# A PEER transformer block on one core: eight more early down products, low parts moved inside a head, the last two up products by token block

## The chip, the core and the metric

The kernel runs on one core of one Trainium2 chip. TensorE (PE) multiplies, ScalarE (ACT) copies and applies functions, VectorE (DVE) does elementwise work and the sorted lists, GpSimd (POOL) does elementwise work and issues indirect DMAs, SyncE (SP) issues plain DMAs. Each engine works through its own list of instructions in order; engines wait for each other on semaphores. The metric is the device time of one launch in microseconds.

## The reference

One block of a streaming encoder: a token mixer (window attention and gated units, not touched here), then a PEER channel mixer on 512 tokens of width 1024:

```python
q = (xt @ w_query).reshape(T, PEER_HEADS, 2, D_HALF)          # 8 heads, two halves of 128
s = jnp.einsum('thpd,hpnd->thpn', q, sub_keys)                 # 128 keys for each half
top_s, top_i = lax.top_k(s, PEER_TOPK)                         # 16 of 128, each half
cand = top_s[:, :, 0, :, None] + top_s[:, :, 1, None, :]       # 16 x 16 sums
best_s, best_c = lax.top_k(cand.reshape(T, 8, 256), PEER_TOPK) # the picks of a head
ids = i1 * N_KEYS + i2                                         # 128 of 16384 experts a token
gates = softmax(best_s)
a   = jnp.einsum('tkd,td->tk', expert_down[ids], xb)
act = gelu(a) * gates
y   = jnp.einsum('tk,tkd->td', act, expert_up[ids])
x   = x + gt2 * rms_norm(y, g)
```

## The kernel before

**Dense for three blocks, gathered for one.** The tokens lie in four blocks of 128. For the first three (384 tokens) the kernel multiplies with all experts, in 128 tiles of 128 experts: a *down product* (`multiply_down`, n = 0 to 127) gives a tile's activations, gelu follows, they are multiplied with the dense gate matrix of the picks, and an *up product* (`multiply_up`) adds the tile's output into six PSUM banks. Each float32 operand is split into a high part (`dhi`, `uhi`, `ahi`, a rounding copy on ScalarE) and a low part (`dlo`, `ulo`, `alo`, a subtraction on VectorE), and a product is three matmuls for each pair of parts: a down product is 24 matmuls of 384 columns, an up product 18 of 512. For the fourth block the 128 picked rows of each token are gathered by GpSimd, one pick at a time (`gather_down`, `gather_up`); VectorE makes a dot product (`dot`) and adds a weighted row into y (`add_up`), in groups of `SLOTS` = 3 picks (`gathered`).

**Heads.** For head h, TensorE makes queries and scores in two halves; VectorE sorts them. `halves(h)` takes the 16 best of each half (`top16`), `sums(h)` the 16 best of the sums, then adds up the chosen keys of head h - 1 (`select`), and ends with the numbers `pairf` of head h (signal `dve_pair`). GpSimd's `weigh_hits(h)` waits for `dve_pair`; it makes two differences, then `split_wq(h + 2, 1)`, the low part of the query weights that TensorE needs for the second half of the queries of head h + 2, then two products, then `split_wq(h + 3, 0)`. TensorE's order in a head, and ScalarE's, with two early down products:

```python
def head(h, first=False):                # TensorE
    for s in range(2):
        queries(h, (s,))
        multiply_down(2 * h - 2 + s, s, first=first)
    scores_of(h, (0, 1))
# ScalarE: query copies, query weights' high parts, early(2h-2+s), score copies, hits(h-1)
```

Down product n needs `dlo` of n. There are two buffers for each kind of tile: the high part of tile n + 2 (`down_hi` in `early(n)`) waits until down product n has ended, and the load of tile n + 2 (`next_down(n)` on SyncE) waits for the low part of tile n. `store_gel(n)`, which keeps an early tile's gelu in DRAM, stands behind `next_down(n)` in SyncE's list and waits for gelu n. So the load of tile n + 3 is behind gelu n.

**Picks.** After the last head VectorE makes the softmax and the last sums, ScalarE an exp and `hits(7)`, TensorE three sets of transposes. **Gates.** 24 turns (`gates_turn`) follow: two gate products and one early down product a turn; ScalarE copies the gates to `stage` and stores them to `gates_dram` in six chunks of 64 tokens, the last chunk in four stores. Before the change 46 tiles are early: 16 in heads, 6 around the picks (`BETWEEN`), 24 in the gates' turns.

**Rounds.** The other 82 tiles run in 41 rounds: TensorE does down a, up r of the early tiles (slot 0), down a + 1, then the up products of slots 1 and 2 of the round before. VectorE does three activations, three pairs of low parts, two low parts of down tiles and one group of picks (`gathered(r, k)`). The remaining early tiles' up products stand behind the rounds; before the change seven up products follow the last round. Each loads its tile, its gate rows and its gelu (`gbuf`).

**The end.** y of the fourth block is normalised when its last add is done, then the three dense blocks, one after another, as their banks are finished.

## Time and profile before

| | us |
|---|---|
| median of three runs (1597.95 to 1600.35) | 1598.69 |
| the profiled execution | 1596.62 |
| its span, first to last instruction | 1594.8 |

The mean granted clock of TensorE over the span is 0.978 of full speed. The stages in the profiled execution: heads to 459.5 us, picks to 493.5 us (first gate product), gates' turns to 680 us, a pause of TensorE, rounds from 699 us on, the last product at 1583 us, end at 1594.8 us. A timeline row is the start from the span's start, the duration, engine, line, operation, tiles; in brackets the idle time of the engine ahead of it and who ended it. A group's row has busy time and mean duration in ns.

### The profile page before, as it was taken

To read this page: it belongs to the slowest core of one execution; us is meant where nothing else is said; L and a number is where in the kernel's file an instruction comes from. 1 tells how busy PE (TensorE), PEld (TensorE's weight loads), DVE (VectorE), ACT (ScalarE), POOL (GpSimd) and SP (SyncE) were. 2 spreads that over 40 slices of the span, in tenths; PEclk is the share of its full clock that TensorE was granted. 3 is DMA by queue.
4 is the path that set the end of the run, shared out by engine and by line. 5 is a ranking of instruction groups with operands and counts; after the bars stand their busy time and mean duration, and the time that the engine had idled before them with its cause. 6 is when DMAs were issued, how large, how long until landed. Compare 5 with 4: busy or idle time off the path is not lost.

```text
span 1594.8 us, 26301 instructions
## 1 busy us (share of the span) xinstructions
PE 1488.6 (93%) x7670; PEld 1277.6 (80%) x7670; DVE 1194.6 (75%) x2435; ACT 628.5 (39%) x1026; POOL 680.8 (43%) x715
## 2 busy tenths in 40 slices
PE   3999997998769999969999999999999999999994
PEld 3575545987659999958888888888888888888883
DVE  6546437799986788748787777778777787777777
ACT  1114324544346777623333333333333333333322
POOL 0000011566445666626444444455445444445461
PEclk9999998999979999989999999999999999999998
DMA  9962301332124799899999999998999999998984
GB/s 331 361 224 106 106 26 39 102 118 99 55 75 161 203 237 238 229 331 364 309 317 317 314 321 312 311 315 313 318 315 318 311 320 312 314 314 307 312 270 151
DMA packets 248575, 390.55 MB, mean 245 GB/s; under 512 B 119576, under 2 KB 165728, under 8 KB 248416
## 3 DMA queue, kind: packets, MB, share of 16 engines
q1 hardware_dynamic: 112704, 230.50, 42.4%
q0 software_dynamic: 36864, 134.23, 24.1%
q10 hardware_dynamic: 98976, 25.43, 7.0%
q8 instruction: 16, 0.26, 0.1%
q14 instruction: 15, 0.12, 0.0%
HBM read 353.80 MB, written 36.31 MB: 245 GB/s over the span
## 4 chain that ended last, share of the span: by engine, by line
PE 68%; DVE 9%; issue 4%; DMA 1%; ACT 1%; POOL 1%; DVEq 0%; ACTq 0%; POOLq 0%; SPq 0%
PE bank L1668 11%; PE bank L1667 10%; PE bank L1666 10%; PE bank L1609 10%; PE bank L1611 10%; PE bank L1610 10%; PE bank L1644 5%; DVE topi L1156 2%; DVE dlo L1165 1%; DVE top L1153 1%; DVE score L1160 1%; DMA gates_dram<-stage 1%; DVE pick L1176 1%; DVE bests L1153 1%; DMA rows_d<-in_peer_down,idx_d 0%
## 5 line engine op out<-in xcount | busy, mean ns | idle before, releaser
L1609 PE MATMUL bank<-h2hi,dhi 128*128 128x384 f32 x1024 | 348.1, 340 | 32.3 <-DVE dlo L1165 32.3
L1611 PE MATMUL bank<-h2hi,dlo 128*128 128x384 f32 x1024 | 345.1, 337 | 0.0
L1610 PE MATMUL bank<-h2lo,dhi 128*128 128x384 f32 x1024 | 344.6, 337 | 0.0
L1666 PE MATMUL bank<-uhi,ahi 128*128 128x512 f32 x768 | 302.9, 394 | 25.3 <-DVE ulo L1323 25.3
L1668 PE MATMUL bank<-uhi,alo 128*128 128x512 f32 x768 | 304.1, 396 | 0.0
L1667 PE MATMUL bank<-ulo,ahi 128*128 128x512 f32 x768 | 303.4, 395 | 0.0
L1609 PEld LDWEIGHTS bank<-h2hi,dhi 128*128 128x128 f32 x1024 | 194.3, 190 | 38.4 <-DVE dlo L1165 25.0
L610 POOL DMA_INDIRECT rows_u<-in_peer_up,idx_u x128 | 168.7, 1318 | 104.2 <-POOL idx_u L608 97.4
L1165 DVE TENSOR_TENSOR dlo<-down,dhi 128x1024 fp32r<-128x1024 f32 x128 | 179.0, 1399 | 45.4 <-ACT dhi L772 42.0
L1610 PEld LDWEIGHTS bank<-h2lo,dhi 128*128 128x128 f32 x1024 | 194.3, 190 | 4.2
L1611 PEld LDWEIGHTS bank<-h2hi,dlo 128*128 128x128 f32 x1024 | 194.0, 189 | 0.0
L1666 PEld LDWEIGHTS bank<-uhi,ahi 128*128 128x128 f32 x768 | 145.2, 189 | 56.5 <-issue 26.4
L610 POOL DMA_INDIRECT rows_d<-in_peer_down,idx_d x128 | 141.6, 1106 | 99.2 <-POOL idx_d L608 99.2
L1283 DVE SCALAR_TENSOR_TENSOR junk<-rows_d,h2nat 128x1024 f32<-128x1024 f32 x128 | 159.5, 1246 | 27.0 <-DVE y L1295 23.5
L1668 PEld LDWEIGHTS bank<-uhi,alo 128*128 128x128 f32 x768 | 145.1, 189 | 32.8
L1295 DVE SCALAR_TENSOR_TENSOR y<-rows_u,coef,y 128x1024 f32<-128x1024 f32 x128 | 164.0, 1281 | 7.7 <-DMA rows_u<-in_peer_up,idx_u 2.1
L1667 PEld LDWEIGHTS bank<-ulo,ahi 128*128 128x128 f32 x768 | 145.0, 189 | 30.4
L1323 DVE TENSOR_TENSOR ulo<-up,uhi 128x1024 fp32r<-128x1024 f32 x128 | 156.0, 1218 | 1.6 <-ACT uhi L901 1.6
L548 POOL TENSOR_TENSOR wqlo<-wq,wqhi 128x1024 fp32r<-128x1024 f32 x16 | 38.3, 2398 | 266.4 <-ACT wqhi L744 266.4
L608 POOL COPY idx_u<-ids 128x1 uint32 (+1 forms) x128 | 49.1, 384 | 223.8 <-DVE y L1295 223.4
L772 ACT ACTIVATE dhi<-down 128x1024 fp32r<-128x1024 f32 x128 | 134.6, 1053 | 20.5 <-DMA down<-in_down_t 20.4
L1309 DVE TENSOR_TENSOR gel<-gel,gate 128x384 f32<-128x384 f32 x84 | 47.2, 563 | 116.0 <-ACT gel L909 116.0
(203 smaller groups left out, 2196.6 us busy)
## 6 DMA issues: line engine op xcount, KB each, us to landing
down<-in_down_t SPq DMA_DIRECT2D x128, 512.0 KB
up<-in_peer_up SPq DMA_DIRECT2D x128, 512.0 KB, 5.0
ada<-in_w_ada SPq DMA_DIRECT2D x12, 2048.0 KB, 16.3
gate<-gates_dram SPq DMA_DIRECT2D x128, 192.0 KB
gates_dram<-stage ACTq DMA_DIRECT2D x5, 4096.0 KB, 25.3
gel_dram<-gel SPq DMA_DIRECT2D x46, 192.0 KB, 2.1
gele<-gel_dram SPq DMA_DIRECT2D x44, 192.0 KB
wq<-in_peer_query SPq DMA_DIRECT2D x16, 512.0 KB, 4.0
```

The costliest lines, as they stand in the source:

```text
L610: return gp.indirect_dma_start(rows_[k][:], None, table[0], bass.IndirectOffsetOnAxis(ap=idx[k][:, 0:1], axis=0))
L772: act.activation(dhi[s][:], down[s][:], ACT.Copy).then_inc(act_dhi, 1)
L1165: ve.tensor_tensor(dlo[s][:], down[s][:], dhi[s][:].bitcast(F32), ALU.subtract).then_inc(dve_dlo, 1)
L1283: ve.scalar_tensor_tensor(out=junk[:], in0=rows_d[k][:], scalar=1.0, in1=h2nat[:], op0=ALU.mult, op1=ALU.mult, accum_out=dots[:, k:k + 1]) ...
L1295: ve.scalar_tensor_tensor(out=y[:], in0=rows_u[k][:], scalar=coef[:, k:k + 1], in1=y[:], op0=ALU.mult, op1=ALU.add).then_inc(dve_add, 1)
L1323: ve.tensor_tensor(ulo[j][:], up[j][:], uhi[j][:].bitcast(F32), ALU.subtract).then_inc(dve_ulo[j], 1)
L1609: pe.matmul(bank[7 * s][:, 0:TD], dhi[s][:, k, :], h2hi[:, k, 0:TD], start=k == 0, stop=False)
L1610: pe.matmul(bank[7 * s][:, 0:TD], dhi[s][:, k, :], h2lo[:, k, 0:TD], start=False, stop=False)
L1611: last = pe.matmul(bank[7 * s][:, 0:TD], dlo[s][:, k, :], h2hi[:, k, 0:TD], start=False, stop=k == KT - 1)
L1666: pe.matmul(got[:], ahi[j][:, tokens], uhi[j][:, half], start=first, stop=False)
L1667: pe.matmul(got[:], ahi[j][:, tokens], ulo[j][:, half], start=False, stop=False)
L1668: done = pe.matmul(got[:], alo[j][:, tokens], uhi[j][:, half], start=False, stop=last)
```

## The change

It does five things. Four more early down products stand around the picks (`BETWEEN` 6 to 10: tiles 16 to 25) and four behind the gates (`AFTER`: tiles 50 to 53), so that 54 tiles are early and 37 rounds are left. In a head the low parts of down tiles move: `halves(h)` no longer makes those of tiles 2h and 2h + 1; `sums(h)` makes those of tiles 2h + 2 and 2h + 3, behind the list of sums and ahead of `select`. The last chunk's stores (and each chunk's) are issued by ScalarE ahead of `early` of the turn, not behind it. A group of picks is taken one round earlier (`gathered(r + 1, k)` in round r). Behind the rounds 16 early tiles (`LATE`) get their up products one by one, with a pick each until the picks run out; the last two up products are done by token block.

```diff
-PER_HEAD, BETWEEN, TURNS = 2, 6, TD // (2 * TB)
+PER_HEAD, BETWEEN, TURNS, AFTER = 2, 10, TD // (2 * TB), 4
 FIRST_G = IN_HEADS + BETWEEN
-EARLY = FIRST_G + TURNS
+AFTER_G = FIRST_G + TURNS
+EARLY = AFTER_G + AFTER
+LATE = EARLY - ROUNDS - 1
+GROUPS_LEFT = -(-PICKS // SLOTS) - (ROUNDS + 1)
+def late(i):
+    return ROUNDS + 1 + i, i % SLOTS, i // SLOTS + (ROUNDS + 1 if i % SLOTS == 0 else ROUNDS)
...
 # SyncE behind the gates
+            sp.wait_ge(gel_out[0], 16)
             load_gel(0, 0)
+            if AFTER:
+                next_down(AFTER_G, 0)
+                store_gel(AFTER_G, 0)
+                next_down(AFTER_G + 1, 1)
             sp.wait_ge(stored[0], 16 * (CHUNKS // 2))
...
                 load_gate(n, j)
+            for n in range(AFTER_G + 1, EARLY):
+                store_gel(n, n % 2)
+                next_down(n + 1, (n + 1) % 2)
...
 # SyncE behind the rounds
+            for i in range(SLOTS, LATE):
+                n, j, use = late(i)
+                sp.wait_ge(dve_act[j], use)
+                load_gate(n, j)
+                sp.wait_ge(dve_ulo[j], use)
+                load_up(n, j)
+                load_gel(n, j)
...
 # ScalarE around the picks
-            for s in range(2):
-                early(IN_HEADS - 2 + s, s)
+            for s in range(4):
+                early(IN_HEADS - 2 + s, s % 2)
             act.wait_ge(dve_bsub, 1)
...
             hits(PH - 1)
             for s in range(2):
-                early(IN_HEADS + s, s)
+                early(IN_HEADS + 2 + s, s)
+            for s in range(2):
+                early(IN_HEADS + 4 + s, s)
...
 # ScalarE, a turn of the gates
+                    for u in range(2):
+                        gates_out(w, i, u)
+                        if t < TURNS - 1:
+                            hot_rows(2 * t + u + 2, u)
+                    if i == TURNS_C - 1:
+                        store_turns(w)
+                    early(FIRST_G + t, t % 2)
...
+            for n in range(AFTER_G, EARLY - 2):
+                early(n, n % 2)
             parts_hi(0, 0, first=True)
+            for n in range(max(AFTER_G, EARLY - 2), EARLY):
+                early(n, n % 2)
...
 # VectorE, heads
-            def halves(h):
-                for s in range(2):
-                    down_lo(2 * h + s, s)
+            def halves(h, last=False):
+                for s in range(2):
+                    if last and s == 1:
+                        for n in range(IN_HEADS, IN_HEADS + 2):
+                            down_lo(n, n % 2)
...
                 top16(lambda b: cand[:, b], lambda b: bests[:, b, :], lambda b: besti[:, b, :])
+                for s in range(2):
+                    down_lo((IN_HEADS if final else 2 * h) + 2 + s, s)
                 if not first:
                     select(h - 1)
...
             ve.tensor_tensor(pick[:, 2], best[:], first, ALU.subtract).then_inc(dve_bsub, 1)
             for s in range(2):
-                down_lo(IN_HEADS + s, s)
+                down_lo(IN_HEADS + 4 + s, s)
             ve.wait_ge(act_gexp, 1)
...
 # VectorE behind the gates
+            if AFTER:
+                down_lo(AFTER_G, 0)
             ch.link(ve.memset(y[:], 0.0))
+            if AFTER:
+                gathered(0, 0, first=True)
+                gathered(0, 1, first=True)
+                down_lo(AFTER_G + 1, 1)
+                gathered(0, 2, first=True)
+                for n in range(AFTER_G + 2, EARLY):
+                    down_lo(n, n % 2)
+                loaded_activations(0, 0, 1)
+                parts_lo(0, 0)
...
 # VectorE behind the rounds
+            late_activations(0)
+            for i in range(LATE):
+                if i + 1 < LATE:
+                    late_activations(i + 1)
+                q, k = ROUNDS + 1 + i // SLOTS, i % SLOTS
+                if q <= ROUNDS + GROUPS_LEFT:
+                    gathered(q, k, last=SLOTS * q + k >= PICKS)
+                n, j, use = late(i)
+                parts_lo(j, use)
...
 # TensorE
-            for n in range(IN_HEADS - 2, IN_HEADS + 2):
+            for n in range(IN_HEADS - 2, IN_HEADS + 6):
                 multiply_down(n, n % 2)
             pe.wait_ge(dve_pick, 1)
...
+            for n in range(AFTER_G, EARLY):
+                multiply_down(n, n % 2)
...
+            def multiply_up_last(slots):
+                for j, c in slots:
+                    up_ready(j, c)
+                for b in range(GB):
+                    for j, c in slots:
+                        for q in (2 * b, 2 * b + 1):
+                            done = up_part(j, q, last=j == slots[-1][0])
+                            if j == slots[-1][0]:
+                                done.then_inc(pe_y, 1)
```

## Rows read from the trace of the kernel before

**Rows 1.** The page: busy time, share of the span, instructions.
```profile
PE 1488.6 (93%) x7670; PEld 1277.6 (80%) x7670; DVE 1194.6 (75%) x2435; ACT 628.5 (39%) x1026; POOL 680.8 (43%) x715
```

**Rows 2.** Busy time by stretch: a head, the picks, behind the gates, the rounds.
```profile
core 0: us, PE busy (x) PEld busy (x) DVE busy (x) ACT busy (x) POOL busy (x), PEclk, DMA share, GB/s
334.00:358.00 24.00, 23.82 (x128) 21.18 (x128) 23.36 (x115) 12.68 (x17) 15.26 (x6) 1.00 0.35 114
456.00:494.00 38.00, 29.03 (x158) 29.00 (x159) 26.05 (x44) 17.22 (x26) 16.74 (x10) 0.81 0.33 110
680.00:700.00 20.00, 5.10 (x27) 4.62 (x26) 4.95 (x6) 3.21 (x6) 3.07 (x3) 0.72 1.10 309
1200.00:1400.00 200.00, 200.00 (x981) 177.33 (x980) 158.05 (x201) 71.02 (x105) 97.09 (x116) 1.00 0.91 315
```

**Rows 3.** Timeline of VectorE, heads and picks: start, us, what [idle before <-releaser].
```profile
283.58 0.23 DVE L1215 TENSOR_TENSOR pairf<-place,start 128x64 f32<-128x64 f32 x1
...
292.90 0.88 DVE L1153 MAX8 top<-score 128x8 f32<-128x128 f32 x4 [7.89 <-ACT score L796]
...
297.59 1.40 DVE L1165 TENSOR_TENSOR dlo<-down,dhi 128x1024 fp32r<-128x1024 f32 x1
...
310.29 0.21 DVE L1195 CAST topf<-topi 128x128 f32<-128x128 uint32 x1
...
312.47 0.23 DVE L1215 TENSOR_TENSOR pairf<-place,start 128x64 f32<-128x64 f32 x1
...
410.94 2.85 DVE L1165 TENSOR_TENSOR dlo<-down,dhi 128x1024 fp32r<-128x1024 f32 x1 [0.23 <-issue]
...
434.88 0.22 DVE L1215 TENSOR_TENSOR pairf<-place,start 128x64 f32<-128x64 f32 x1
...
459.28 0.22 DVE L1215 TENSOR_TENSOR pairf<-place,start 128x64 f32<-128x64 f32 x1
...
471.12 2.35 DVE L1176 TENSOR_REDUCE pick<-hit 128x64 f32<-128x1024 f32 x2 [2.27 <-POOL hit L564]
```

**Rows 4.** Timeline of GpSimd, the turn after head 1.
```profile
312.87 4.82 POOL L556 TENSOR_TENSOR hit<-pairf,iota 128x1024 f32<-128x1024 f32 x2 [9.26 <-DVE pairf L1215]
...
317.64 2.42 POOL L548 TENSOR_TENSOR wqlo<-wq,wqhi 128x1024 fp32r<-128x1024 f32 x1
```

**Rows 5.** Timeline of ScalarE, heads and picks.
```profile
291.26 1.05 ACT L772 ACTIVATE dhi<-down 128x1024 fp32r<-128x1024 f32 x1
...
350.10 1.06 ACT L772 ACTIVATE dhi<-down 128x1024 fp32r<-128x1024 f32 x1 [3.81 <-DMA down<-in_down_t]
...
466.99 1.28 ACT L778 ACT_TABLE_LOAD   x1
```

**Rows 6.** Timeline of TensorE: a head, gates, behind them, the tail.
```profile
323.25 0.39 PE L1554 MATMUL bank<-h2hi,wqhi 128*128 128x512 f32 x1
...
328.73 0.33 PE L1609 MATMUL bank<-h2hi,dhi 128*128 128x384 f32 x1
...
493.47 0.72 PE L1644 MATMUL bank<-gated,onehot 128*128 128x128 f32 x5
...
698.93 0.77 PE L1666 MATMUL bank<-uhi,ahi 128*128 128x512 f32 x1 [14.90 <-DVE ulo L1323]
...
1568.70 0.77 PE L1666 MATMUL bank<-uhi,ahi 128*128 128x512 f32 x1 [7.60 <-DVE ulo L1323]
```

**Rows 7.** Timeline of SyncE's DMA queue, a head.
```profile
345.46 0.34 SPq L423 DMA_DIRECT2D down<-in_down_t  x1
```

**Rows 8.** Timeline of ScalarE's DMA queue, the last stores of the gates.
```profile
680.40 12.64 ACTq L868 DMA_DIRECT2D gates_dram<-stage  x3
```

**Rows 9.** The page: the group of adds of gathered rows on VectorE.
```profile
L1295 DVE SCALAR_TENSOR_TENSOR y<-rows_u,coef,y 128x1024 f32<-128x1024 f32 x128 | 164.0, 1281 | 7.7 <-DMA rows_u<-in_peer_up,idx_u 2.1
```

**Rows 10.** DMA issues by line: size, median us to landing.
```profile
gel<-gel_dram SPq DMA_DIRECT2D x2, 192.0 KB, 6.9
```

**Rows 11.** Timeline of VectorE, the last low part.
```profile
1572.17 1.23 DVE L1323 TENSOR_TENSOR ulo<-up,uhi 128x1024 fp32r<-128x1024 f32 x1 [0.39 <-ACT uhi L901]
```

More of the change, by code:

```diff
@@ L858, in gates_out @@
                         ACT.Copy).then_inc(act_g, 1)
-            def gates_turn(w, i, e, last=False):
-                for u in range(2):
-                    gates_out(w, i, u)
-                    if not last:
-                        hot_rows(2 * (TURNS_C * w + i) + u + 2, u)
-                early(FIRST_G + TURNS_C * w + i, e)
             def store_chunk(w, keys_1, signal):
@@ L920, in round_ @@
                     down_hi(a + 2, 0)
-                if not first:
-                    gelu_dots(r, SLOTS * r)
+                gelu_dots(r + 1, SLOTS * r + SLOTS)
                 parts_hi(0, r + 1)
@@ L1177, in select, with sums @@
                                      in_=hit[s][:], axis=AXX, op=ALU.add).then_inc(dve_sel, 1)
-            def sums(h, first=False):
+            def sums(h, first=False, final=False):
                 ch.wait()
@@ L1222, in _ @@
                 sums(h)
-                ch.leave(PH - 1)
+                ch.leave(PH - 2)
+            halves(PH - 1, last=True)
+            sums(PH - 1, final=True)
             first = best[:, :, :, 0:1].broadcast_to([P, NB, PH, TOPK])
@@ L1260, in _ @@
                 hot_rows(u, u)
-            for n in range(IN_HEADS + 4, FIRST_G + 1):
+            for n in range(IN_HEADS + 8, FIRST_G + 1):
                 down_lo(n, n % 2)
@@ L1330, in round_ @@
                 loaded_activations(0, r + 1, r + 2)
[L1331 removed]
+                gathered(r + 1, 0)
                 parts_lo(0, r + 1)
@@ L1630, in _ @@
                 last.then_inc(pe_pick, 1)
-            for n in range(IN_HEADS + 2, FIRST_G):
+            for n in range(IN_HEADS + 6, FIRST_G):
                 multiply_down(n, n % 2)
@@ L1690, in _ @@
                 multiply_up(j, ROUNDS - 1)
-            multiply_up(0, ROUNDS + 1)
-            for j in range(1, SLOTS):
-                multiply_up(j, ROUNDS)
-            multiply_up(0, ROUNDS + 2, last=True)
+            for i in range(LATE - 2):
+                n, j, use = late(i)
+                multiply_up(j, use)
+            multiply_up_last([late(i)[1:] for i in (LATE - 2, LATE - 1)])
 _INS = ["x", "c", "w_ada", "b_ada", "g_pre_mix", "g_post_mix", "g_pre_ffn", "g_post_ffn", "w_in", "attn_sinks",
```

116 lines of the change are left out of this document (53 added, 63 removed).

## The prediction

> **What bounds the kernel now.** I read the page first: TensorE is busy 93% of the span, VectorE 75% [rows 1]. A share is an average, so I read the busy time stretch by stretch [rows 2]. In the rounds (1200 to 1400 us) TensorE shows no gap: 200 us for 981 matmuls, 0.204 each. A round has 5 products (2 downs of 24 matmuls, 3 ups of 18, together 102), so it takes 20.8 us, and a product 4.16. VectorE has 42 us in 200 to spare there, the DMA engines are busy 0.91. Time is lost in the head stretch (VectorE busy 23.36 of 24), around the picks (TensorE 29.0 of 38, clock 0.81) and behind the gates (TensorE 5.1 of 20).
>
> Then the timelines. VectorE's gives the ends of the numbers: head 0 at 283.8, head 1 at 312.7, head 6 at 435.1, head 7 at 459.5 [rows 3]: 24.4 us a head. From head 7 to the first gate product it is 34.0 us [rows 3, 6].
>
> **The ideal.** Eight downs leave the rounds: 8 x 4.16 = 33.3 us. They pay only where they fall into time in which TensorE stands. So each stage is summed by itself.
>
> **Heads 0 to 6.** Off: two low parts at a head's start, beside GpSimd, 2.85 us each where shown; on: two behind the list of sums, where I expect them near the 1.23 us that the same subtraction takes alone [rows 3, 11]. That is 3.2 us less for VectorE: 24.4 becomes 21.2. TensorE needs about as much: two query halves of 5.5 (323.25 to 328.73 [rows 6]), two downs of 4.16, scores at some 2 (an estimate). But the moved low parts carry a new wait. `sums(h)` now makes the low part of tile 2h + 3, which needs its `dhi`; that waits until down product 2h + 1 has ended, which stands in TensorE's head h + 1 behind the second query half; that half waits for `split_wq(h + 1, 1)`, and GpSimd makes that behind `pairf` of head h - 1. So from one `pairf` to the next:
> - GpSimd's two differences and the split: the split ends at 320.05, 7.35 behind `pairf` at 312.7 [rows 4];
> - the query half 5.5 [rows 6] and the down 4.16, with 0.3 for the hops: 10.0;
> - the gelu 0.4 (an estimate) and `dhi` 1.05 [rows 5];
> - the low part 1.2, `select` 2.25 and the numbers 2.4 (310.29 to 312.70) [rows 3].
>
> Together 24.65 us a head, 0.25 over now. Behind the wait stand `select` and the numbers on VectorE; GpSimd waits for these, and TensorE's next half for GpSimd: the loop closes. Head 0 also shifts: its numbers need no `dhi` now; after, they stand behind that of tile 3, ready at 292.3 [rows 5]. Low part 1.2 and numbers 2.4 put them at about 296.0, not 283.8. Then 296.0 + 6 x 24.65 = 443.9 against 435.1: **+8.8**. TensorE is then idle some 3.4 us ahead of each second half (24.65 - 21.2). A granted clock below full speed behind a pause is seen at 456 to 494 us and behind the gates [rows 2]; for five such heads I add **+2** (bounds: 0, and 5 x 1.3 = 6.5, if the product behind each pause takes a third longer; an estimate).
>
> What speaks for the load of tile 2h + 3 being in time: landed loads are in use 4.6 us behind their issue (345.46 to 350.10 [rows 7, 5]), and its issue waits only for gelu 2h, a half head earlier.
>
> **Head 7.** The last head makes the low parts of tiles 16 and 17 ahead of the second half's lists. `dhi` 17 needs the load of 17, which is behind `store_gel(14)`, so behind gelu 14, which ScalarE does behind `hits(6)`. From `pairf` 6: differences 4.8 [rows 4], ScalarE's two passes 2.3 and the gelu 0.5 (estimates near [rows 5]'s 1.05 for a pass), issues 0.6, landing 4.6 [rows 7, 5], `dhi` 1.05, low part 1.2: 16.1. Then the second lists (4.7, as 292.90 to 297.59), sums and `select` (1.40 and 4.7 off 297.59 to 310.29 leave 6.6), two low parts 2.4, numbers 2.4 [rows 3]: 16.1. Together 32.2, less 0.4 where the passes overlap the differences: 31.8 against 24.4, **+7.4** (bounds: 0 if the load comes in time, +10 if GpSimd stretches it).
>
> **Picks.** Behind `pairf` 7: first difference 2.6, exp 0.6, `hits(7)` four passes 4.4, table load 1.3 [rows 5], a gelu (18) 0.5, issues 0.6, landing 4.6, `dhi` (21) 1.05, low part 1.2, softmax sums 2.9, `select` 2.35 [rows 3]: 22.1; ids 0.6, low part of 22 1.2: 23.9; four downs 16.6: 40.5, against 34.0. The small operations are estimates. The downs 18 to 21 lie in this time, beside VectorE's work; the four from 22 on do not, where two stood before. **+6.5**. The bounds are -4 (all cover) and +10.
>
> So the first gate product starts about 24.7 later, at 518, with 26 tiles early instead of 22.
>
> **Behind the first gate product**, against before:
> - four downs less to do, 4 x 4.16, and the last two products start together, one place earlier: **-16.6 and -4.2**.
> - The pause behind the gates. Before, TensorE waited 14.9 us for up 0 and restarted slowly [rows 6, 2]; about 16.8 in all. The four new downs (50 to 53) should fill it. But ScalarE's list now has the last chunk's stores ahead of `early`. Before, three of them took 12.64 us to issue [rows 8]. If ScalarE stands for that, gelu 49 and `dhi` 51 come 12 to 14 us late, down 51 starts some 10 us behind the end of 50, and `store_gel(49)` holds SyncE, which loads the next tiles: about 16 us of pause stay, **-0.8** (bounds -12 and +4).
> - The late tiles. Now 16 up products stand behind the rounds, 4.16 each on TensorE. VectorE's step for each is an activation and gate product (two of 0.5), a low part 1.2, an add 1.28 [rows 9], a dot product 1.25: 4.8 with the low part of the activation. It is over 4.16, and the loop of a buffer is longer: gelu rows land 6.9 us behind their issue [rows 10], issued behind the low part (0.5), then 4.9 of work, over the two steps in between: 12.3 / 2 = 6.15. I take 5.5, between them: 16 x (5.5 - 4.16) less what the first steps have in hand gives about 18 us of idle. Before, the seven tail products lost about 12.7: the wait of 7.6 [rows 6], and smaller ones (698.93 to 1568.70 is 869.8 for 206 products, 857.0 by 4.16: 12.8 in all, some 2.4 of it in the rounds; and an estimated 2 of slow clock behind the wait). **+5.3** (bounds -5 and +14).
> - The end. Before, the last low part ended at 1573.4 [rows 11] with one product running and two queued, and the rest was hidden behind them. Now both last products wait for it, and the end is 1594.8 - 1573.4 = 21.4 from it where 15.8 stood from the last product's start: **+5.6**.
>
> Sum: -16.6 - 4.2 - 0.8 + 5.3 + 5.6 = **-10.7**.
>
> **Total.** 8.8 + 2 + 7.4 + 6.5 - 10.7 = +14. The profiled execution took 1596.62 (span 1594.8 and 1.8 around it) and becomes 1610.6; the median of the runs is 2.1 above the profiled one, so **1612.5**.
>
> **Rivals.** *The loop in the heads doesn't hold* (the other side). If down 2h + 1 ends before the list of sums does, the moved low parts wait for nothing and a head is 21.2: 6 x 3.2 = 19 less than now, less head 0's shift of 12.2, and TensorE's slow restarts fall away: about -9 in place of +10.8, and the cover for heads 7 and picks is better by some 5. That gives 1612.5 - 20 - 8 = about 1585. It decides at one point: whether `dhi` of 2h + 3 is ready when the list of sums ends. For it speaks VectorE's 23.36 of 24 [rows 2]; against it the sum of the loop, whose terms are all rows but one. The Trainium skill (SBUF — State Buffer, Who interferes with whom) says that a VectorE instruction with two SBUF inputs contends with a GpSimd instruction that reads SBUF; the trace agrees, 2.85 against 1.23 for one low part. By that rule alone, with no wait, the move would pay by the 3.2 us a head just named.
>
> *The stores don't hold ScalarE.* Then down 51 follows at once, the pause falls from 16 to about 7: 1603.5. The row of 12.64 shows the queue's time to issue, and no ScalarE instruction that waits behind it. The Trainium skill (Perfetto Trace Analysis, DMA Instruction — HWDGE) has the sequencer in use until the descriptors are generated; no row here shows it for ScalarE, and by it the pause stays.
>
> *The late steps go at VectorE's price.* At 4.8 a step the tail loses 10 less: 1602. At 6.15 it loses 10 more: 1622.
>
> *It doesn't matter.* The ideal of 33.3 cancels the losses of heads and picks only if the pause and tail both come out at their low bounds: within 3.2 us (0.2%, about what a measurement can tell) of 1598.7.
>
> **The numbers.** The forecast with its own bounds: 0.70. A short pause or quick tail, but still slower: 0.12. Both at low bounds, no change: 0.07. The head rival: 0.11, faster. Faster 0.11, same 0.07, slower 0.82. The range takes in the short pause, the quick tail (1602) and the slow tail (1622), and goes 2 us towards the case in which both come out low: 1600 to 1622.
>
> **What the profile after would show.** Low parts of 1.2 us in the heads, with a wait of some 3 to 4 us for `dhi` ahead; TensorE waiting ahead of each second query half for `wqlo`; ends of the numbers at 296, 320.7, 443.9 and 475.7; the first gate product near 518; an issue of some 12 us ahead of ScalarE's gelu 49; VectorE waiting for a load in the late steps. If the waits in the heads are missing, the first step is wrong; if the numbers of head 6 end before 435, the whole forecast is.

## The result, and the profile after

The changed kernel takes 1616.82 us in the median of four runs (1610.96 to 1619.35), the kernel before 1598.67 in its four (1597.95 to 1600.35): a ratio of 1.0111, 95% interval 1.0096 to 1.0126, so it is about 18 us slower. The forecast was 1612.5, with a range of 1600 to 1622. The profiled execution took 1617.37, with a span of 1615.6; 1610.6 was forecast for it.

In the order of the prediction, first the heads. VectorE's timeline of the changed kernel, the numbers (L1238), the low parts (L1184) and the small adds into `cand` (L1204):

```profile
293.16 1.23 DVE L1184 TENSOR_TENSOR dlo<-down,dhi 128x1024 fp32r<-128x1024 f32 x1 [8.44 <-ACT dhi L790]
296.50 0.23 DVE L1238 TENSOR_TENSOR pairf<-place,start 128x64 f32<-128x64 f32 x1
320.86 0.23 DVE L1238 TENSOR_TENSOR pairf<-place,start 128x64 f32<-128x64 f32 x1
341.75 1.22 DVE L1184 TENSOR_TENSOR dlo<-down,dhi 128x1024 fp32r<-128x1024 f32 x1 [2.07 <-ACT dhi L790]
347.33 0.23 DVE L1238 TENSOR_TENSOR pairf<-place,start 128x64 f32<-128x64 f32 x1
357.38 3.86 DVE L1204 TENSOR_TENSOR cand<-top 128x192 f32<-128x192 f32 x3
390.24 2.34 DVE L1184 TENSOR_TENSOR dlo<-down,dhi 128x1024 fp32r<-128x1024 f32 x2
421.33 0.23 DVE L1238 TENSOR_TENSOR pairf<-place,start 128x64 f32<-128x64 f32 x1
440.91 1.23 DVE L1184 TENSOR_TENSOR dlo<-down,dhi 128x1024 fp32r<-128x1024 f32 x1 [3.06 <-ACT dhi L790]
446.49 0.23 DVE L1238 TENSOR_TENSOR pairf<-place,start 128x64 f32<-128x64 f32 x1
459.80 1.23 DVE L1184 TENSOR_TENSOR dlo<-down,dhi 128x1024 fp32r<-128x1024 f32 x1 [2.91 <-ACT dhi L790]
476.93 0.22 DVE L1238 TENSOR_TENSOR pairf<-place,start 128x64 f32<-128x64 f32 x1
486.74 1.23 DVE L1184 TENSOR_TENSOR dlo<-down,dhi 128x1024 fp32r<-128x1024 f32 x1 [8.99 <-ACT dhi L790]
```

The rows answer to [rows 3]. Head 0 ends at 296.7 (forecast 296.0), head 6 at 446.7 (443.9), head 7 at 477.2 (475.7). The low parts are short, 1.2 us (two in one row, 2.34), and some wait for `dhi`. But the wait is 8.4 us in head 0, 2.1, 0.8 and 3.1 in heads 2, 3 and 6, and absent in heads 1, 4 and 5 (as at 390.24): in these VectorE is full. What fills it is new: the three adds into `cand` take 3.86 us together. In the kernel before they took 0.62, on its VectorE:

```profile
352.74 0.62 DVE L1183 TENSOR_TENSOR cand<-top 128x192 f32<-128x192 f32 x3
```

GpSimd's timeline of the changed kernel at the same place, against [rows 4]:

```profile
347.72 3.84 POOL L574 TENSOR_TENSOR hit<-pairf,iota 128x1024 f32<-128x1024 f32 x2 [13.17 <-DVE pairf L1238]
351.51 2.36 POOL L566 TENSOR_TENSOR wqlo<-wq,wqhi 128x1024 fp32r<-128x1024 f32 x1
353.82 4.74 POOL L582 TENSOR_TENSOR hit<-hit,topf 128x1024 f32<-128x1024 f32 x2
358.48 2.55 POOL L566 TENSOR_TENSOR wqlo<-wq,wqhi 128x1024 fp32r<-128x1024 f32 x1
```

The adds run from 357.4 to 361.2. The second product of GpSimd ends at 358.6 and the split for a first half runs from 358.5 to 361.0, so the adds stand beside both. In head 6, which has no split for a first half, they take 1.56 us.

Of heads 1 to 6, those with a wait for `dhi` are those in which TensorE ran at the lower of its two clock levels for a while. One stretch for each of heads 1 to 6, TensorE's busy time and its granted clock (PEclk):

```profile
296.70:321.10 24.40, 24.36 (x128) 1.00 0.31 104
321.10:347.60 26.50, 23.46 (x110) 0.87 0.28 94
347.60:372.80 25.20, 22.88 (x114) 0.93 0.30 99
372.80:397.20 24.40, 22.08 (x118) 1.00 0.31 102
397.20:421.60 24.40, 21.38 (x114) 1.00 0.29 102
421.60:446.70 25.10, 22.16 (x117) 0.93 0.17 57
```

In heads 2 to 6 TensorE waits 2.3 to 3.0 us for `wqlo` ahead of the second query half. At the full clock that half then takes 5.5 us (heads 4 and 5), with some 3.4 us at the half clock 7.1 (heads 3 and 6), with 6.8 us of it 8.3 (head 2). TensorE's timeline, against [rows 6]: a second query half that waits for the split, the first gate product, two waits behind the gates, and the last two up products:

```profile
327.56 0.76 PE L1600 MATMUL bank<-h2hi,wqhi 128*128 128x512 f32 x1 [3.04 <-POOL wqlo L566]
...
516.81 3.40 PE L1690 MATMUL bank<-gated,onehot 128*128 128x128 f32 x29
...
722.19 0.69 PE L1655 MATMUL bank<-h2hi,dhi 128*128 128x384 f32 x1 [14.81 <-DVE dlo L1184]
731.57 0.45 PE L1655 MATMUL bank<-h2hi,dhi 128*128 128x384 f32 x1 [3.19 <-DVE dlo L1184]
...
1594.31 0.47 PE L1711 MATMUL bank<-uhi,ahi 128*128 128x512 f32 x1 [0.55 <-DVE ulo L1350]
```

ScalarE's timeline behind the gates, against [rows 8]: the four stores' issue, then gelu 49.

```profile
699.69 19.65 ACTq L881 DMA_DIRECT2D gates_dram<-stage  x4
719.44 0.49 ACT L796 ACTIVATE gel<-bank 128x384 f32<-128x384 f32 x1 [19.78 <-issue]
```

VectorE's waits from 1500 us on, and its last low parts and adds:

```profile
DVE gel L1336 <- DMA gel<-gel_dram: 12.0, 9, 3.0
DVE gele L1336 <- DMA gele<-gel_dram: 4.4, 4, 1.8
```

```profile
1529.06 1.22 DVE L1350 TENSOR_TENSOR ulo<-up,uhi 128x1024 fp32r<-128x1024 f32 x1
...
1587.95 1.22 DVE L1350 TENSOR_TENSOR ulo<-up,uhi 128x1024 fp32r<-128x1024 f32 x1
...
1592.94 1.22 DVE L1350 TENSOR_TENSOR ulo<-up,uhi 128x1024 fp32r<-128x1024 f32 x1
1594.27 2.61 DVE L1322 SCALAR_TENSOR_TENSOR y<-rows_u,coef,y 128x1024 f32<-128x1024 f32 x2
```

Where the 20.8 us between the two spans (1615.6 and 1594.8) come from:

| stretch | forecast | measured |
|---|---|---|
| to the end of head 6 | +10.8 | +11.6 (446.7, 435.1) |
| head 7 | +7.4 | +6.0 (30.4, 24.4) |
| picks | +6.5 | +5.7 (39.7, 34.0) |
| first gate product to the last product's start (before), to the last pair's (after) | -16.3 | -7.9 (1077.5, 1085.4) |
| from there to the end | +5.6 | +5.4 (21.3, 15.9) |
| sum | +14 | +20.8 |

The 1085.4 run to the kernel before's last product, whose first matmul is this row of its TensorE:

```profile
1578.91 0.39 PE L1666 MATMUL bank<-uhi,ahi 128*128 128x512 f32 x1
```

Five products fewer lie in the fourth stretch, 20.8 us, but only 7.9 show, so 12.9 are lost again. The rounds are not the place: a round takes 20.81 us in both kernels. 5.2 of the 12.9 are at the pause: waits of 14.8 and 3.2, a product that took 6.2 in place of 4.16, and behind the second wait three products in 14.2 in place of 12.5, 22.0 in all against 16.8. The other 7.7 are lost behind the rounds: 19 products in 99.3 us (20.2 over their own time), where the kernel before has 8 in 45.8 (12.5 over).

### The profile page after: what moved, and what is told of

It is laid out like the page before. It is cut to its first block, busy times and chain, and to the rows that moved or that the text cites. A ratio compares the mean times of both kernels' runs of the same rounds, so it can differ in the third digit from the quotient of the medians.

```text
span 1615.6 us, 25769 instructions
## 1 busy us (share of the span) xinstructions
PE 1501.6 (93%) x7670; PEld 1285.9 (80%) x7670; DVE 1186.9 (73%) x2435; ACT 626.4 (39%) x1026; POOL 676.6 (42%) x715
## 4 chain that ended last, share of the span: by engine, by line
PE 64%; DVE 8%; DMA 4%; issue 3%; ACT 2%; ACTq 1%; POOL 1%; SPq 0%; DVEq 0%; POOLq 0%
PE bank L1655 10%; PE bank L1657 10%; PE bank L1656 10%; PE bank L1713 9%; PE bank L1712 9%; PE bank L1711 9%; PE bank L1690 5%; DMA gel<-gel_dram 2%; ACTq L881 1%; DVE pick L1197 1%; DVE y L1322 1%; PE bank L1600 1%; DMA gele<-gel_dram 1%; PE bank L1601 1%; PE bank L1602 1%
## 5 line engine op out<-in xcount | busy, mean ns | idle before, releaser
L1655 PEld LDWEIGHTS bank<-h2hi,dhi 128*128 128x128 f32 x1024 | 195.8, 191 | 40.5 <-DVE dlo L1184 37.1
L1184 DVE TENSOR_TENSOR dlo<-down,dhi 128x1024 fp32r<-128x1024 f32 x128 | 157.1, 1230 | 94.6 <-ACT dhi L790 94.6
L628 POOL DMA_INDIRECT rows_u<-in_peer_up,idx_u x128 | 175.1, 1368 | 104.2 <-POOL idx_u L626 97.4
L1711 PEld LDWEIGHTS bank<-uhi,ahi 128*128 128x128 f32 x768 | 145.1, 189 | 49.7 <-issue 19.8
L1310 DVE SCALAR_TENSOR_TENSOR junk<-rows_d,h2nat 128x1024 f32<-128x1024 f32 x128 | 159.0, 1242 | 25.5 <-DVE y L1322 21.3
L626 POOL COPY idx_u<-ids 128x1 uint32 (+1 forms) x128 | 55.8, 436 | 232.0 <-DVE y L1322 231.5
```

The costliest lines, as they stand in the source:

```text
L628: return gp.indirect_dma_start(rows_[k][:], None, table[0], bass.IndirectOffsetOnAxis(ap=idx[k][:, 0:1], axis=0))
L1184: ve.tensor_tensor(dlo[s][:], down[s][:], dhi[s][:].bitcast(F32), ALU.subtract).then_inc(dve_dlo, 1)
L1310: ve.scalar_tensor_tensor(out=junk[:], in0=rows_d[k][:], scalar=1.0, in1=h2nat[:], op0=ALU.mult, op1=ALU.mult, accum_out=dots[:, k:k + 1]) ...
L1655: pe.matmul(bank[7 * s][:, 0:TD], dhi[s][:, k, :], h2hi[:, k, 0:TD], start=k == 0, stop=False)
L1711: pe.matmul(got[:], ahi[j][:, tokens], uhi[j][:, half], start=first, stop=False)
```

## The experiments

Two theories stood at the start. One: the moved low parts close a loop through the split, the second query half, a down product and its `dhi`, and it sets the heads. The other: the moved low parts are free or pay, and the front's loss is that of the downs more around the picks. All ratios are to the kernel before in the same set of runs (its medians there are 1597.6 to 1598.7). The intervals of runs 2, 5, 8 and 11 touch or overlap that of the changed kernel, so what they gain or lose against it, 2.5 to 8 us, is at the edge of what the medians can tell.

| run | median us | ratio (95% interval) | head 2's end to head 5's, a head | first gate product |
|---|---|---|---|---|
| before | 1598.67 | | 24.49 | 493.5 |
| changed | 1616.82 | 1.0111 (1.0096 to 1.0126) | 24.67 | 516.8 |
| 1 low parts only | 1608.51 | 1.0066 (1.0052 to 1.0080) | 24.95 | 505.0 |
| 2 old front | 1610.66 | 1.0085 (1.0071 to 1.0098) | 24.49 | 509.8 |
| 3 split first | 1609.57 | 1.0076 (1.0062 to 1.0089) | 24.86 | 509.8 |
| 4 odd part back | 1606.97 | 1.0056 (1.0042 to 1.0070) | 24.37 | 505.6 |
| 5 split waits for sums | 1611.40 | 1.0084 (1.0071 to 1.0097) | 24.19 | 511.7 |
| 6 both | 1599.34 | 1.0011 (1.0002 to 1.0020) | 22.14 | 497.5 |
| 7 stores by SyncE | 1607.72 | 1.0065 (1.0052 to 1.0078) | 24.92 | 512.1 |
| 8 gelu rows earlier | 1609.12 | 1.0085 (1.0070 to 1.0099) | 24.36 | 513.3 |
| 9 before, splits moved | 1599.51 | 1.0011 (1.0002 to 1.0020) | 24.53 | 494.9 |
| 10 old front, new rest | 1597.68 | 0.9998 (0.9989 to 1.0007) | 24.49 | 494.5 |
| 11 last two one by one | 1614.29 | 1.0102 (1.0087 to 1.0117) | 24.67 | 516.7 |
| 12 mended | 1586.40 | 0.9928 (0.9914 to 0.9941) | 22.14 | 498.8 |

Runs 7, 8 and 11 have the changed kernel's code up to the gates, and their first gate product still comes at 512.1, 513.3 and 516.7. So the front with the low parts moved differs by some 5 us from one execution to the next, and a difference of that size in one profile proves nothing. Most of it is there by the end of head 6 (442.6, 444.8 and 446.8, against 446.7 in the changed kernel; 1.2 of run 7's 4.1 is there at head 0), and it goes with TensorE's clock. A head in which TensorE stays at the full clock takes 24.3 to 24.4 us in all of them (head 6: 23.6 in run 7), one with some 3.4 us at the half clock 25.1 to 25.3, one with 6.8 us 26.5. Run 7 has two slow heads (4 and 5), run 8 has two (2 and 6), the changed kernel and run 11 have three (2, 3 and 6), with 6.8 us in head 2. The wait ahead of the second half is 2.2 to 3.1 us in slow and in full heads alike, so the rows don't show what decides which.

**1. The low parts alone**, in the kernel before. The orders of the last head and of the picks go with them.

```diff
 # VectorE, sums(h), behind the list of sums
+                for s in range(2):
+                    down_lo((IN_HEADS if final else 2 * h) + 2 + s, s)
 # halves(h)
-                    down_lo(2 * h + s, s)
```

> The kernel before with the moved low parts alone: six early downs around the picks, 41 rounds, the old order behind the gates and the old end. Theory (the loop through the split, the second query half, the down product and its high part closes at 25.0 us a head): head 0 ends at about 296.5, head 6 at 446 to 447, head 7 at about 477, each as in the changed kernel; the first gate product starts at about 500 (516.8 less four downs of 4.16), 6.7 us later than before, and the time is about 1605.5. Rival (the moved low parts are free or pay, the four downs more around the picks are what the front costs): head 6 at 435 or earlier, the first gate product at 489 or earlier, the time 1594 or less.

Head 6 ends where the loop theory had it:

```profile
447.20 0.23 DVE L1221 TENSOR_TENSOR pairf<-place,start 128x64 f32<-128x64 f32 x1
504.97 6.55 PE L1653 MATMUL bank<-gated,onehot 128*128 128x128 f32 x32 [4.34 <-DVE gated L1265]
```

The gates start 11.5 us later than before, not 6.7: without four downs there, TensorE also waits 4.3 us for the first one-hot rows, and starts its gate products slowly (6.55 us for 32; 3.7 in the changed kernel). The median rises by 10.6 us. The move alone makes the kernel slower; that the low parts are free or pay is out. What the four downs more cost, this run can't say.

**2. The old front**, ten downs around the picks. The last head and the picks go back to the old order too.

```diff
-                    down_lo((IN_HEADS if final else 2 * h) + 2 + s, s)
+                    down_lo(2 * h + s, s)          # in halves(h)
```

> The changed kernel with heads and picks in the old order (low parts at a head's start and between its halves; only downs 14 to 17 ahead of the transposes), but still ten early downs around the picks, four behind the gates and the new end. Theory: head 6 ends at 435, head 7 at 459.5 as before, the first gate product at 493.5 + 4 x 4.16 = 510.1, 6.7 us earlier than in the changed kernel, the rest unchanged: about 1610. Rival (the front's order costs nothing): first gate product at 516 or later, 1616.8.

The gates start at 509.8 and the time is 1610.7, as the theory had it. Four downs more cost 16.4 of their 16.6 us there: with the old order none of them is hidden.

**3. The split ahead of the wait for the numbers.**

```diff
+                if splits[1]:
+                    split_wq(h + 2, 1)
                 gp.wait_ge(dve_pair, h + 1)
...
                 gp.wait_ge(dve_top, h + 1)
-                if splits[1]:
-                    split_wq(h + 2, 1)
```

> The changed kernel with one thing moved: GpSimd makes the split of the query weights for the second half of head h + 2 ahead of its wait for the numbers of head h, not behind the two differences. That opens the loop and leaves all else. Theory: the waits of VectorE for dhi and of TensorE for wqlo in the heads vanish, a head takes 21.2 to 21.8 us in place of 25.0, head 6 ends at 424 to 428, the first gate product starts about 20 us earlier (495 to 499) and the time is about 1596. Rival (a head is bound by VectorE's or TensorE's own work and the loop is only an accident of it): head 6 ends within 3 us of 446.7 and the time stays at 1616.8.

A miss, and the most useful one. The waits for `dhi` in heads 2 to 5 are gone, but heads 3 to 5 take 24.9 us each, not 21.2. Rows of VectorE and of GpSimd:

```profile
379.19 4.40 DVE L1204 TENSOR_TENSOR cand<-top 128x192 f32<-128x192 f32 x3
```

```profile
378.56 4.83 POOL L566 TENSOR_TENSOR wqlo<-wq,wqhi 128x1024 fp32r<-128x1024 f32 x2
```

The adds now stand beside two splits instead of one and grow to 4.4 us; they end with the splits. VectorE is full again. The split was moved to a place beside the adds, so this run opens the loop and lengthens the adds at once. The loop isn't the only bound, and the theory needed a second part: the 3.2 us saved at the low parts are lost at the adds into `cand`. Of the 7 us that the run gains, 4 come at head 6, which takes 21.1 (418.9 to 439.9 in its numbers), where GpSimd has no split for a first half left to make.

**4. Only the even low part moved**, with the old order of the last head and the picks.

```diff
-                    down_lo((IN_HEADS if final else 2 * h) + 2 + s, s)
+                down_lo(2 * h + 2, 0)
...
+                    if s == 1:
+                        down_lo(2 * h + 1, 1)      # in halves(h)
```

> The changed kernel with only the even low part behind the list of sums; the odd one goes back to between the halves of the next head, and the picks have the old order. The even one's dhi is ready long before, the odd one's wait was the one that closed the loop. Theory: a head loses 1.7 us against the kernel before (2.9 becomes 1.2 for one low part) and takes about 22.7, head 6 ends at about 421 to 423, head 7 at about 444 to 446, the first gate product at 494 to 497, and the time is about 1595. Rival (low parts behind the list of sums delay the numbers whichever they are): a head takes 24.4 or more, head 6 ends at 435 or later, the time is 1610 or more.

A miss too: 24.4 a head, not 22.7. The even part takes 1.21 us, the odd one 2.4, and the adds 2.7: together 6.3, against 2.9 + 3.0 + 0.6 = 6.5 in the kernel before. What contention is left only changes its place. It is 10 us faster than the changed kernel, mainly because head 0 no longer waits for `dhi` 3: its numbers start their last step at 286.5, where they do at 296.5. Head 1 gives 3.2 of that back, heads 2 to 6 win 5.9 more, and the last head and the picks together take 1.5 longer.

**5. The split waits for the sums.**

```diff
                 if splits[0]:
+                    gp.wait_ge(dve_half, h + 2)
                     split_wq(h + 3, 0)
```

> The changed kernel with one wait more on GpSimd: the split for the first half of head h + 3 waits until VectorE has made the sums of head h + 1 (the adds into cand). In the changed kernel that split (2.5 us) runs at the same time as these three small adds, which take 3.8 to 3.9 us against 0.61 in the kernel before. Theory (an addition with two SBUF inputs stands still while GpSimd's split runs, so that the time saved at the low parts goes back there): the adds take 0.6 to 0.7 us, VectorE's own work falls to 21.2 us a head, and the loop through the other split is left as the bound, by the changed kernel's rows 3.84 + 2.36 + 0.3 for differences and split, 5.5, 4.5, 1.45, 1.2, 2.3 and 2.4: 23.7 to 23.9 us a head. Head 6 ends at about 439 in place of 446.7 and the time is about 1609. Rival (the adds are slow for another reason, or the head is bound elsewhere): adds of 3.8, head 6 within 2 us of 446.7.

The adds fall to 1.70 us, not 0.6: they still stand beside the end of GpSimd's second product (to 405.6). Heads 4, 5 and 6 take 23.7, 23.7 and 23.6, as the sum made for this run has it; the low part waits 1.4 us for `dhi` there:

```profile
404.40 1.70 DVE L1205 TENSOR_TENSOR cand<-top 128x192 f32<-128x192 f32 x3
412.45 1.22 DVE L1185 TENSOR_TENSOR dlo<-down,dhi 128x1024 fp32r<-128x1024 f32 x1 [1.44 <-ACT dhi L791]
```

Heads 2 and 3 take 25.3 and 25.2, with waits of 3.1 and 3.0 us for `dhi` and a granted clock of 0.93. So with the adds shorter the loop is the bound in every head from 1 to 6, at 23.7 us with TensorE at the full clock and 1.5 to 1.6 more where its second query half runs slow. Head 6 ends at 441.8, not 439, by those two heads. The time, 1611.4, is near the 1609 expected.

**6. Both edits.**

> The last kernel with the other split moved as well: both splits stand ahead of the wait for the numbers and behind the sums. With the split moved alone the adds took 4.4 us, a head 24.9, and VectorE had no wait left. Theory: with neither the loop nor the adds in the way a head takes 21.3 to 22.5 us (VectorE's own 21.2, and up to 1.2 more where the second split meets a low part), head 6 ends at 424 to 432 and the time is 1596 to 1602. Rival (VectorE's loss only moves on, now to the low parts behind the lists): a head of 24 us or more, head 6 at 440 or later, 1609.

```profile
385.33 0.22 DVE L1239 TENSOR_TENSOR pairf<-place,start 128x64 f32<-128x64 f32 x1
395.38 0.61 DVE L1205 TENSOR_TENSOR cand<-top 128x192 f32<-128x192 f32 x3
399.70 3.40 DVE L1185 TENSOR_TENSOR dlo<-down,dhi 128x1024 fp32r<-128x1024 f32 x2
407.46 0.23 DVE L1239 TENSOR_TENSOR pairf<-place,start 128x64 f32<-128x64 f32 x1
```

22.1 us a head, adds of 0.61, and two low parts in 3.40 (1 us of it beside a split). The time falls by 17.5 us against the changed kernel. Loop open alone 24.9, adds free alone 24.2, both 22.1: two bounds of nearly one length lay over each other, and either edit alone shows the other bound. Against run 2, with the same ten downs around the picks, this front starts the gates 12.3 us earlier and the median is 11.3 us lower: that is what the moved low parts are worth once both bounds are gone.

**7. The last chunk's stores by SyncE.**

```diff
 # ScalarE
-                    store_chunk(w, slice(0, 16), stored_part[0])
...
 # SyncE, behind next_down(AFTER_G, 0)
+            sp.wait_ge(act_g, CHUNKS * (CHUNK_T // 4))
+            store_part(slice(0, 16), stored_part[0])
+            store_part(slice(EARLY, EARLY + 16), stored_part[0])
...
 # SyncE, behind round_(0) and behind round_(1)
+            store_part(slice(16, EARLY), stored_part[1])
+            store_part(slice(EARLY + 16, KEYS), stored_part[1])
```

> The changed kernel with the last chunk's four stores issued by SyncE: two behind the load of tile 52, the other two behind rounds 0 and 1. In the changed kernel ScalarE stands 19.8 us behind them, gelu 49 comes at 719.4 and TensorE waits 14.8 and 3.2 us. Theory (the issue of the stores holds ScalarE's list): gelu 49 comes at about 700.5, down 51 follows down 50 at once, and what is left is SyncE's own issue of two stores (some 5 us each) ahead of the load of tile 53 and the landing of the gates; 8 to 12 us off, time 1605 to 1609. Rival (the 4 MB of stores and the loads behind them set the pause whoever issues them): less than 3 us off, 1614 or more.

ScalarE is free and TensorE's waits behind the gates fall from 14.8 and 3.2 to 2.2 and 7.1; the second fits SyncE's next issues, which are slow behind its stores:

```profile
701.70 4.79 SPq L482 DMA_DIRECT2D gates_dram<-stage  x2
706.52 5.50 SPq L434 DMA_DIRECT2D gel_dram<-gel  x1
712.07 1.33 SPq L430 DMA_DIRECT2D down<-in_down_t  x1
```

1607.7, within what the theory said. From the first gate product to the end it is 1088.2 us; the changed kernel has 1098.8, and the five other runs with its code there (2 to 6) 1094.4 to 1097.9. The pause loses 11.7 us here and 19.3 to 22.6 in those six. So 8 to 11 us come from here, and the median falls by 9.1.

**8. Late gelu rows earlier.**

```diff
+                sp.wait_ge(dve_alo[j], use)
+                load_gel(n, j)
                 sp.wait_ge(dve_ulo[j], use)
                 load_up(n, j)
-                load_gel(n, j)
```

> The changed kernel with the late tiles' loads in another order: SyncE loads the next gelu rows as soon as the low part of the activation is made, ahead of the wait for the low part of the up tile. Theory (the buffer's loop, 12.3 us over two steps, sets the step of the late tiles, measured 5.9): the loop is 1.2 to 1.7 us shorter, a step 5.2 to 5.4, ten steps give 5 to 7 us and the time is about 1611. Rival (VectorE's own work of 4.85 a step, or the DMA engines' load, sets it): within 2 us of 1616.8.

Ten steps from 1518.17 to 1572.15 are 5.40 each, where the changed kernel has ten from 1529.06 to 1587.95 at 5.89. But these are not the same steps of the row, and they differ between executions. The same ten (up to the last low part but two) are 5.51 us each here and 5.89 in the changed kernel, and 5.43 to 5.96 in the other runs with sixteen late tiles in the old order (2 to 7 and 11). VectorE's waits from 1500 us on are now short and of several kinds:

```profile
DVE y L1323 <- DMA rows_u<-in_peer_up,idx_u: 4.9, 5, 1.8
DVE gel L1337 <- DMA gel<-gel_dram: 2.5, 2, 1.8
```

The waits for gelu rows are nearly gone, but in the ten steps VectorE still idles 9.1 us, where it has 8.0 to 13.4 with the old order: waits for gathered rows have taken their place. Behind the rounds TensorE loses 14.4 us here (15.7 in run 12, which has the same edit), against 16.6 to 22.1 in the changed kernel and runs 2 to 7. From the first gate product to the end it is 1092.3 us, against 1094.4 to 1098.8 in the changed kernel and runs 2 to 6. So the edit helps by some us, but how much isn't shown: the median fell by 7.7 with single times from 1607.4 to 1615.1.

**9. The splits moved in the kernel before**, the edits of runs 3 and 5 with the low parts in their old places.

> The kernel before, low parts in their old places, with GpSimd's two splits moved as in the run that took 22.1 us a head (both behind the sums, ahead of the wait for the numbers). Theory (the moved low parts do save VectorE 3 us a head, once nothing else is put beside GpSimd): here the low parts still stand beside GpSimd's differences and products at 2.9 to 3.0 us each, VectorE stays full and a head takes 24.0 to 24.6; head 7 ends at 457 to 461 and the time is within 3 us of 1597.6. Rival (the gain of that run came from GpSimd's order alone): 22.1 a head, head 7 at 443 to 446, 1585 or less.

24.5 a head, low parts of 2.9 and 3.0 us, adds of 0.61: the theory's case. GpSimd's order alone is worth nothing; the moved low parts pay only together with it.

**10. The old front with the new rest.**

```diff
-PER_HEAD, BETWEEN, TURNS, AFTER = 2, 10, TD // (2 * TB), 4
+PER_HEAD, BETWEEN, TURNS, AFTER = 2, 6, TD // (2 * TB), 4
```

(with the edit of run 2).

> The changed kernel with the front of the kernel before (low parts, picks, six downs around the picks), so that only the work behind the first gate product is changed: four downs behind the gates, stores ahead of early, 39 rounds, ten late tiles, the last two by token block. Theory from the rows of both kernels: first gate product at 493.5; as many products to the last one's start but one, -4.2; the pause behind the gates loses 20 us against 16.6, +3.6; ten late steps at 5.9 lose about 17 against 12.7, +4; from the last product's start to the end 21.3 against 15.8, +5.5; together +9, about 1606.5. Rival (the new order behind the gates is worth its four downs, and all the loss is the front's): 1594 or less.

Neither: no change (0.9998), where theory had 8 us of loss and the rival a gain. TensorE's waits behind the first gate product:

```profile
PE bank L1645 <- DVE dlo L1182: 16.0, 2, 13.4
PE bank L1701 <- DVE ulo L1340: 8.1, 8, 1.7
```

The pause loses 19.0 us (16.0 waited, and a product of 6.7), not 20, against 16.8 before. Ten late tiles cost less than I priced: behind the rounds TensorE loses 9.7 us, less than the 12.5 of the kernel before, where the changed kernel's sixteen lose 20.2. The waits are 8.1 against 15.0, and the changed kernel has 6.8 us at the half clock there, this run none. The last eight steps before the pair (1530.58 to 1572.11) are 5.2 each, the same eight of the changed kernel 5.4, of run 3 5.2: the step itself doesn't show a growth with the number of late tiles.

Runs 10 and 2 differ only in the four downs more around the picks, and these cost 13.0 us (1597.68 to 1610.66; 9.9 between the two profiles). The gates start 15.4 us later, and behind them only 5.5 of the four products' 16.6 come back, because six more tiles are late (20.5 us lost there, against 9.7). The moved low parts add the last 6.2 (run 2 to the changed kernel, at the edge of the noise). So the larger part of the 18 us is the downs around the picks, though the low parts cost 10.6 without them. Run 12's front with six downs around the picks was not tried.

**11. The last two up products one by one.**

```diff
-            for i in range(LATE - 2):
+            for i in range(LATE - 1):
                 n, j, use = late(i)
                 multiply_up(j, use)
-            multiply_up_last([late(i)[1:] for i in (LATE - 2, LATE - 1)])
+            multiply_up_last([late(LATE - 1)[1:]])
```

> The changed kernel with its last two up products one after the other. Theory (from the last low part on the end hangs on VectorE's list, y's two adds, its norm and three blocks at 3.4 us each, and TensorE's banks are ready before their turn): no difference, 1616.8 within the 4 us that executions of this kernel differ by, and 21.3 to 21.5 us from the end of the last low part to the end of the span, as with the pair by token block. Rival (the token blocks hide part of the end): 2 to 4 us more than 21.4 from the last low part to the end.

No difference: intervals 1.0087 to 1.0117 and 1.0096 to 1.0126 overlap. The last low part ends at 1592.97 and the span at 1614.4, 21.4 us; with the pair by token block 1594.16 and 1615.6, 21.4 too; in the kernel before 1573.4 and 1594.8 [rows 11], 21.4 again. The end follows the last low part at the same distance, whatever TensorE's order is, as the theory of VectorE's list has it.

**12. The three edits together** (6, 7 and 8).

> The changed kernel with the three edits that helped, together: both splits behind the sums and ahead of the wait for the numbers, the last chunk's stores by SyncE, the late gelu rows loaded behind the activation's low part. Alone they took off 17.5, 9.1 and 7.7 us. They act in three stretches (heads, behind the gates, behind the rounds), so theory has them add up: 1582 to 1586, faster than the kernel before by 12 to 16 us. Rival (what one gives back is lost at the next, as at the adds in the heads; or the faster front meets the DMA engines at their limit behind the gates): 1590 or more.

```profile
417.94 0.61 DVE L1214 TENSOR_TENSOR cand<-top 128x192 f32<-128x192 f32 x3
428.96 0.23 DVE L1248 TENSOR_TENSOR pairf<-place,start 128x64 f32<-128x64 f32 x1
```

```profile
696.39 0.44 PE L1665 MATMUL bank<-h2hi,dhi 128*128 128x384 f32 x1 [2.84 <-DVE dlo L1194]
707.95 0.69 PE L1665 MATMUL bank<-h2hi,dhi 128*128 128x384 f32 x1 [5.53 <-DVE dlo L1194]
```

1586.4 us, 0.9928 of the kernel before (0.9914 to 0.9941): 11.7 us faster than it in the same set of runs, 30.4 under the changed kernel's median. The edits' gains one by one sum to 34.3, so they nearly add up; the time is just over the 1582 to 1586 expected. It beats both kernels.

## Why the prediction was right, and where it was off

- **The sign and the size.** Slower was forecast at 0.82, 1612.5 was 4.3 us too low, and 1616.8 lies in the range. The profiled execution was 6.8 us over its forecast; the median is less far off because it lies 0.5 below the profiled time here and not 2.1 above. The mechanism was right in part: two of its prices in the heads were wrong and cancelled each other.
- **Head 0's shift.** Right: 296.7 against 296.0, with the wait of 8.4 us for `dhi` 3.
- **"Together 24.65 us a head" (the loop).** It exists: run 1 shows the loss by itself, and run 5 shows it as the bound. But at the full clock it is 23.7 us long, 1 less than I summed, since GpSimd's differences now take 3.84 where [rows 4] had 4.82. That is under VectorE's own 24.4, so in the changed kernel it sets only heads 2 and 3, in which TensorE's second query half ran slow, and head 6, in which the adds are short. The waits of 3 to 4 us for `dhi` that the profile was to show are 2.1, 0.8 and 3.1 there, and missing in three heads.
- **"I add +2" for the clock.** Measured: six heads at VectorE's 24.38 are 146.3 us, and heads 1 to 6 took 150.0 (446.7 - 296.7), 3.7 more. The slow halves cost 2.1, 0.9 and 1.6 us of that, and head 6 gives 0.8 back (at the full clock it takes 23.6, run 7), all within the bounds of 0 and 6.5. The forecast for the same stretch was 6 x 24.65 + 2 = 149.9. That it is right to 0.1 is luck.
- **"That is 3.2 us less for VectorE: 24.4 becomes 21.2."** This step failed. The low parts did get short, but the adds into `cand` grew from 0.6 to 3.9 us, since a split of GpSimd's and the end of a product now run beside them. VectorE's own price stayed about 24.4, and the forecast came out because the loop, which was to be the longer of the two, had been priced at nearly that (24.65). It also undoes the rival that the head falls to 21.2: run 3 opened the loop and got 24.9. I had taken the short adds of before as a property of theirs, and hadn't asked what would stand beside them.
- **The Trainium skill's rule** (SBUF — State Buffer, Who interferes with whom), that a VectorE instruction with two SBUF inputs contends with a GpSimd instruction that reads SBUF, and that the port pair they share is an exclusive lock: the trace agrees, since the adds end 0.2 us behind the one split (361.2 and 361.0), in run 3 behind both (383.6 and 383.4), and in run 5 0.5 us behind the product (406.1 and 405.6). In the prediction it was read for the low part alone, where it should have been asked of every two-input operation in the head.
- **Head 7 and picks.** 31.8 forecast, 30.4 measured; 40.5 and 39.7. The first terms of head 7 were added up wrong: as listed they make 15.05, not 16.1, and the head 30.8; the rows have 14.3 for them (446.7 to 461.0). The chains through the gelu, its store and the next load are in the rows: waits of 2.9 and 9.0 us for `dhi`.
- **The pause, "about 16 us stay".** The mechanism was right: ScalarE stood 19.8 us behind the stores' issue and gelu 49 came at 719.4. Run 7 took the stores off ScalarE and won 8 to 11 us, so the rival in which they don't hold it is out. The size was off by 6.0 (22.0, and 5.2 over before where -0.8 was forecast): the issue of four stores took 19.7 us, not the 12 to 14 that I worked out from three in 12.64, and a second product waited and restarted slowly as well. The Trainium skill (Perfetto Trace Analysis, DMA Instruction — HWDGE) has the sequencer in use until the descriptors are generated; the trace agrees, with 19.78 us of idle named "issue".
- **The late tiles, "I take 5.5".** Mis-sized, and less so: 7.7 us more lost than before, not 5.3. Ten steps are 5.89 in this profile, between 5.5 and the upper bound of 6.15, and 5.43 to 5.96 in others with the same code there. The waits for gelu rows (16.4 us in 13) show the buffer's loop at work; run 8 shows that the gathered rows are a bound of nearly the same length behind it.
- **Two smaller slips.** 1610.6 and 2.1 make 1612.7, not 1612.5. The head rival's own terms make -7 for the heads, not -9, and 5 for the cover, not 8: about 1590, not 1585.
- **The end, +5.6.** Measured +5.4, and the last pair does wait for the last low part (0.55 us, at 1594.31). From the last low part to the end it is 21.4 us in both kernels, so the +5.4 says only that the last products start later against that low part.

What stays open: what decides in which heads TensorE restarts at the lower clock, how much of run 8's gain is its own, and what the mended front gives with six downs around the picks.

## What to carry to other kernels

When an operation is moved away from a neighbour that slows it, ask what moves in beside that neighbour: here 3 us were saved at two large subtractions and lost at three tiny adds. When a chain of waits and an engine's own work have nearly one length, mending one shows little; test them together before giving either up. Give a chain that runs through TensorE two lengths, one for each clock level, because it may be the bound at one and not at the other (23.7 and 25.2 us here, beside 24.4 of VectorE's own). An engine that issues large strided stores does nothing else meanwhile (19.8 us here): put them on a list in which nothing behind them is due soon.

## What was not expected of the hardware

Three adds of up to 192 columns, 0.61 us by themselves, took 1.6 to 1.7 beside the end of one GpSimd product, 3.8 to 3.9 beside that and a subtraction of 1024 columns (2.55 us), and 4.4 beside two subtractions. The second query half took 5.5, 7.1 or 8.3 us behind waits of much the same length, by the granted clock. The issue of four strided stores on ScalarE's queue held ScalarE for 19.8 us (17.4 to 20.5 in other runs), and a small store by SyncE behind two of them took 5.50 us to issue where such a one takes 0.35.
